# Split products of unchanged activation parts, written to a bank that nobody reads, in six waits of the norm chains

## The reference

```
lat = lat + mod_l[:, 2] * rms_norm(y_lat, norm_g[i, 1])
h   = modulate(rms_norm(lat, norm_g[i, 2]), mod_l[:, 3], mod_l[:, 4])
lat = lat + mod_l[:, 5] * rms_norm(swiglu(h, ffn_w_in[i], ffn_w_out[i]), norm_g[i, 3])
...
h = x * (1.0 + scale_t) + shift_t;  proj = h @ w_in[l]
x = layernorm(DEEPNORM_ALPHA * x + gate_t * mix, ln1_g[l], ln1_b[l])
h = x * (1.0 + scale_f) + shift_f;  u = causal_dwconv(h @ w_up[l], conv_ffn[l]) + b_conv_ffn[l]
x = layernorm(DEEPNORM_ALPHA * x + gate_f * ffn, ln2_g[l], ln2_b[l])
```

## Time and profile before

| | |
|---|---|
| median of 3 runs | 1017.96 us |
| lowest, highest | 1012.38, 1018.58 us |
| profiled execution, first to last instruction | 1009.4 us |
| mean granted TensorE clock in it | 0.977 |
| TensorE matmul busy | 943.4 us (93%) |
| VectorE busy | 702.2 us (70%) |
| ScalarE busy | 548.3 us (54%) |
| DMA: mean rate, bytes moved | 195 GB/s, 196.78 MB |

### The profile page before, as it was taken

The page is one execution under the profiler, slowest core; times in us unless marked ns, Lnnn a source line. Parts: engine busy times, 40 slices in busy tenths (PEclk is TensorE's granted clock), DMA queues, the critical chain, the costliest instruction groups (busy, mean ns, idle before and its releaser), DMA issues.

```text
span 1009.4 us, 19912 instructions
## 1 busy us (share of the span) xinstructions
PE 943.4 (93%) x8438; PEld 891.3 (88%) x8438; DVE 702.2 (70%) x1112; ACT 548.3 (54%) x829; POOL 28.5 (3%) x71
## 2 busy tenths in 40 slices
PE   4699999979999999799999999999999799999995
PEld 1479999859999999699888999988899599999994
DVE  2649936757877766797875544466688678988744
ACT  2658232655544543766746344566765566766434
POOL 2100000000000000310100000000000000000000
PEclk9799999999999999899999999999999899999998
DMA  9834664637888888357433437353386345556931
GB/s 332 293 110 131 224 253 169 209 124 248 276 286 302 285 284 304 104 166 253 146 126 107 167 108 202 122 185 129 117 317 230 110 147 188 188 188 191 340 96 42
DMA packets 57400, 196.78 MB, mean 195 GB/s; under 512 B 6096, under 2 KB 10592, under 8 KB 57056
## 3 DMA queue, kind: packets, MB, share of 16 engines
q1 hardware_dynamic: 51840, 187.72, 55.2%
q10 hardware_dynamic: 5216, 7.53, 2.7%
q0 software_dynamic: 256, 0.26, 0.1%
HBM read 194.43 MB, written 1.06 MB: 194 GB/s over the span
## 4 chain that ended last, share of the span: by engine, by line
PE 76%; DVE 15%; ACT 5%; issue 2%; DMA 2%; ACTq 0%; SPq 0%; DVEq 0%
PE panel_banks L402 64%; DVE mix_work L1807 3%; DVE w_lo L1465 3%; PE work_banks L772 2%; ACT w_hi L950 2%; DMA raw<-in_panels 2%; PE work_banks L599 1%; PE work_banks L743 1%; DVE gla_work L1582 1%; DVE raw L1498 1%; PE work_banks L559 1%; PE work_banks L532 1%; PE work_banks L855 1%; PE work_banks L800 1%; ACT gla_work L988 0%
## 5 line engine op out<-in xcount | busy, mean ns | idle before, releaser
L402 PE MATMUL panel_banks<-act_hi,w_hi 128*128 128x256 f32 (+1 forms) x1600 | 461.9, 289 | 23.1 <-DVE w_lo L1465 8.8
L402 PE MATMUL panel_banks<-act_hi,w_lo 128*128 128x256 f32 (+1 forms) x1600 | 453.3, 283 | 0.0
L402 PE MATMUL panel_banks<-act_lo,w_hi 128*128 128x256 f32 (+1 forms) x1600 | 453.3, 283 | 0.0
L1465 DVE TENSOR_TENSOR w_lo<-raw,w_hi 128x1024 fp32r<-128x1024 f32 x260 | 315.4, 1222 | 126.1 <-ACT w_hi L950 123.9
L950 ACT ACTIVATE w_hi<-raw 128x1024 fp32r<-128x1024 f32 x260 | 272.7, 1055 | 152.0 <-PE panel_banks L402 112.5
L402 PEld LDWEIGHTS panel_banks<-act_hi,w_hi 128*128 128x128 f32 x1600 | 304.9, 191 | 36.8 <-issue 22.2
L402 PEld LDWEIGHTS panel_banks<-act_hi,w_lo 128*128 128x128 f32 x1600 | 306.1, 191 | 1.6
L402 PEld LDWEIGHTS panel_banks<-act_lo,w_hi 128*128 128x128 f32 x1600 | 304.9, 191 | 2.1 <-issue 0.5
L402 PE MATMUL panel_banks<-hidden_hi,w_hi 128*128 128x256 f32 x352 | 97.7, 277 | 2.5 <-ACT hidden_hi L1169 2.5
L402 PE MATMUL panel_banks<-hidden_hi,w_lo 128*128 128x256 f32 x352 | 97.4, 277 | 0.0
L402 PE MATMUL panel_banks<-hidden_lo,w_hi 128*128 128x256 f32 x352 | 97.4, 277 | 0.0
(11 more groups left out here) (268 smaller groups left out, 961.5 us busy)
## 6 DMA issues: line engine op xcount, KB each, us to landing
raw<-in_panels SPq DMA_DIRECT2D x356, 512.0 KB, 5.1
mix_work<-delta_rows ACTq DMA_DIRECT2D x2, 1024.0 KB, 14.6
x_t<-in_x ACTq DMA_DIRECT2D x1, 1024.0 KB, 9.3
gla_work<-in_ctx_x ACTq DMA_DIRECT2D x1, 1024.0 KB, 14.2
mix_work<-in_rel_bias ACTq DMA_DIRECT2D x1, 1024.0 KB, 10.0
out_x<-ffn_work SPq DMA_DIRECT2D x4, 256.0 KB, 2.5
mix_work<-in_rel_bias ACTq DMA_DIRECT2D x1, 768.0 KB, 15.7
c_wide<-in_c_rows ACTq DMA_DIRECT2D x1, 512.0 KB, 4.2
```

The costliest lines, as they stand in the source:

```text
L402: ins = pe.matmul(out_, a, b, start=start and p == 0, stop=stop and p == 2, skip_group_check=True)
L1465: dve.tensor_tensor(wlo[:, v_ % PARTS, :], raw[:, u % RAW, :], whi[:, v_ % PARTS, :].bitcast(F32), ALU.subtract)\
```

## The change

A helper is added on PE that issues n split products with the same operands: weights are the first 128 columns of tile 8 of `act_hi`, the moving operand is tile 9, the result goes to the first 256 columns of bank 3 of the work banks, each product starting its own sum. It waits for nothing and raises no semaphore. It is called in six places ("groups" 1 to 6 in order): 20 products before the squares after gla_out and 20 behind them, 30 behind the sums after ffn_out, 18 between the two sums of the layer norm after mix and 18 behind the second, and 18 between the two sums of the last layer norm: 124 in all.

```diff
+            def idle_products(n):
+
+                for _ in range(n):
+                    pe.matmul(MB[:, 3, 0:T], hhi[:, 8, 0:P], hhi[:, 9, :], start=True, stop=True)
+
...
             norm_part("folded", 0, 3, sq2)
 
+            idle_products(20)
             for r in range(4):
                 if r == 0:
                     pe.wait_ge(S("norm_factor"), 2)
                 norm_part("squares", 4, r, sq2, tiles=2)
+            idle_products(20)
 
             for i in range(22):
                 panel(j, single, ready=None if i else "h2_lo")
...
             for r in range(4):
                 norm_part("folded", 4, r, sq2)
-
+            idle_products(30)
 
             for i in range(12):
                 panel(j, single, ready=None if i else "h3_lo")
...
             norm_part("ln_in", 0, 3, sq2, 0, "ln_sum")
+            idle_products(18)
             for r in range(4):
                 norm_part("folded", 8, r, sq2, 1, "ln_var")
+            idle_products(18)
             for i in range(22):
                 panel(j, single, ready=None if i else "h4_lo")
...
             for r in range(4):
                 norm_part("ln_in", 4, r, sq2, 0, "ln_sum")
+            idle_products(18)
             for r in range(4):
                 norm_part("folded", 12, r, sq2, 1, "ln_var")
```

## The result

| | before | after |
|---|---|---|
| median | 1016.03 us (11 runs) | 1005.67 us (11 runs) |
| lowest, highest | 1008.28, 1022.79 us | 999.31, 1017.27 us |
| profiled execution, span | 1009.4 us | 997.6 us |
| mean granted clock in it | 0.977 | 0.992 |

The ratio is 0.9928 with a 95% interval from 0.990 to 0.9956: 7.3 us less (4.5 to 10.2). It is taken from undisturbed executions alone, so it is not the quotient of the two medians.

A forecast was written before the change was run, and what follows sets the result against it. The prediction saw PE's split products as the bound (76% of the chain), with half clock after waits. Its terms, 0 + 0.8 + 1.4 + 1.45 + 0.35 + 1.43 = 5.4 us off the median 1017.96, gave 1012.6 us, range 1009.0 to 1018.0.

The forecast's parts named there:

- The groups hide in their waits, cost zero: All six groups fit in PE's waits at the high clock with 0.7 to 1.1 us to spare; direct cost zero.
- Slower: Rival, chance 0.08: groups start at the low clock and real products stand behind them; 6.2 us lost, 1024.2 us.
- Group 1, nothing: Squares after gla_out: faster PE gains 0, because the logarithm stands behind ACT's conversion of two weight halves.
- Group 2, half of 1.65: First panel of ffn_in: full clock saves up to 1.65 us; half taken, 0.8, as the clock might still fall.
- Group 3, 1.4: First panel of qkv: 1.8 us earlier at high clock, DVE lets the first convolution move 1.05; 1.4 taken (0 to 1.8).
- Group 4, 1.45: Variance products of the first layer norm, for which ACT, DVE, then PE wait: 1.45 us gained (0 to 1.45).
- Group 5, a quarter of 1.4: First panel of up: up to 1.4 us at stake, a quarter taken, 0.35, as the clock might not hold.
- Group 6, 1.43: Variance products of the last layer norm, with only ACT, DVE and stores behind: 1.43 us gained (0 to 1.43).
- I take the gain off the median: Base of the forecast: the gain taken from the median 1017.96 us, 8.6 over the profiled execution, giving 1012.6.
- All of it: Rival, chance 0.12: the panels of groups 2, 3 and 5 hold fully too; 7.7 us gained, 1010.3 us.
- Only the norm products: Rival, chance 0.25: groups 4 and 6 give 2.9 us, the panels' gain is lost to clock falls or DVE; 1015.1 us.
- nothing: Rival, chance 0.10: products do not keep the clock up, the falls having another cause than idle PE; 1018.0 us.

The follow-up runs named there:

- e2: The changed kernel with only groups 1, 2 and 3, both layer norms as before; median 1011.19 us, ratio to before 0.9984.
- e5: The changed kernel plus tiny products of different kinds behind the float32 norm products within gla_out and mix; 1004.25 us in one execution.
- e8: The changed kernel, unchanged, profiled a second time; 1004.73 us in one execution.
- e9: The changed kernel, unchanged, timed again next to the kernel before; median 1005.86 us (10 runs), ratio to before 0.9952.
- e14: The changed kernel, unchanged, profiled again; 1009.41 us in one execution.
- e15: The changed kernel, unchanged, profiled once more; 1010.30 us in one execution.
- e4: The kernel before, unchanged, profiled a second time; 1012.99 us in one execution, span 1011.2.
- e13: The kernel before, unchanged, its fourth profile; 1009.39 us in one execution.
- e1: The changed kernel with only groups 4, 5 and 6, the two layer norms; median 1006.63 us, ratio to before 0.9957.
- e6: The changed kernel with the same number of added products, each moving 32 columns instead of 256; 1019.15 us in one execution.
- e10: The changed kernel with groups of 24, 27, 34, 20, 23, 18 and a tiny product behind each norm product in gla_out and mix; median 1005.21 us, ratio to before 0.9952.
- e11: The kernel before, without groups, plus a tiny product behind each norm product in gla_out and mix; median 1012.56 us, ratio to before 1.0007.

## Why the prediction was right or wrong

**The groups hide in their waits, cost zero: right.** PE still waits 0.66 to 1.07 us behind them; I had 0.7 to 1.1. They are a little longer than forecast: 2.73 us for 20 and 2.50 for 18, the last one's tail in it, against 2.3 and 2.05. The rival "Slower" needed groups that meet the half clock. In the nine profiles with the groups at the size of the change, or with some of them left out, no product of a group ran at half clock.

**Group 1, nothing: right.** The squares are now done at 218.16 (217.03 + 1.13), but the logarithm stands behind ACT's two weight halves as before. It starts 9.65 us behind the start of the last folded norm product in before (221.44 less 211.79) and 9.67 in after (218.78 less 209.11), by the timelines of ACT and PE. Timeline of ACT in after, which answers to the earlier trace rows:

```profile
216.88 1.99 ACT L960 ACTIVATE w_hi<-raw 128x1024 fp32r<-128x1024 f32 x2
218.78 0.46 ACT L974 ACTIVATE rs<-work_banks,eps 128x256 f32<-128x256 f32 x1
```

**Group 2, half of 1.65: too high.** Where it holds it gives 1.5 to 1.6 (ffn_in 121.1 instead of 122.6), the full term. But of the seven profiles with 20 products there (after, e2, e5, e8, e9, e14, e15) it held in one. On average 0.2, not 0.8. The prediction's own sign of being wrong, a clock that still falls at such a place, came here. Group 2 itself ran at full clock in all seven, and PE waited 1.07 us behind it in each; in six of them the clock fell 1 to 3 us after the first product of the panel.

**Group 3, 1.4: right in kind, 0.4 too high.** The first panel is 1.6 shorter in every profile with the group. The prediction bounded this by DVE at 1.05 and took 1.4 all the same. The first convolution now starts 9.25 us after the layer's first product (418.92 less 409.67), against 10.37 before (424.29 less 413.92): 1.1 earlier, the bound. What the first panel gained beyond it is paid back at the other end of the layer: the last three panels grow from 16.32 to between 16.67 and 17.20 us, and the layer as a whole is 0.8 to 1.3 shorter than 73.5. Timeline of DVE in after, the first convolution, then near the end of qkv:

```profile
418.92 2.68 DVE L1817 SCALAR_TENSOR_TENSOR mix_work<-panel_banks,columns,mix_work 128x255 f32<-128x255 f32 x6
...
474.04 1.23 DVE L1475 TENSOR_TENSOR w_lo<-raw,w_hi 128x1024 fp32r<-128x1024 f32 x1 [0.52 <-ACT w_hi L960]
475.18 2.68 DVE L1817 SCALAR_TENSOR_TENSOR mix_work<-panel_banks,columns,mix_work 128x255 f32<-128x255 f32 x6
477.78 1.22 DVE L1475 TENSOR_TENSOR w_lo<-raw,w_hi 128x1024 fp32r<-128x1024 f32 x1
```

DVE's round of two weight halves and six convolution steps takes some 5.47 us a panel, and PE, which is ahead by the gain, runs into it. One profile of before (e4) had 11.32 and 16.69 without any group; the clock came back earlier there. The mean of qkv is 73.26 in the seven profiles without a group there and 72.45 in the eight with 30 to 34 products, so 0.8 is the fairer value and a little of the 1.0 is chance.

**Group 4, 1.45: right.** Mix is 35.5 to 36.0 without it and 34.2 to 34.7 with it. Its four panels run at one pace or the other, which moves it by 0.3; between profiles with the same paces the difference is 1.36 both times (before 35.74 and after 34.38; e13 36.03 and e15 34.67).

**Group 5, a quarter of 1.4: too low.** It held in seven of the eight profiles that have it (not in e1), and gives 1.5 (up 122.6 to 121.1). I had put it beside group 2 as equally open. The prediction leaned on a clock of 1.00 where group 5 begins. That holds for the one profile read: in the other three of before the clock is at 0.50 over the 4 us ahead of up's first product. Why group 5 nearly always holds and group 2 seldom does is not settled. Both ran at full clock in every profile with wide products.

**Group 6, 1.43: right.** The tail is 17.3 to 17.5 without and 16.15 with it, in every profile with 18 products: 1.1 to 1.35.

**The sum, 5.4 us: right in size.** The terms as measured are 1.4 + 1.35 + 1.0 + 0.2 + 1.3 (1.5 in seven of eight) = 5.25. The second timing gave 4.9, the mean span of five profiles of after is 1004.1 and of four of before 1009.1, and the prediction's own figure for "the same kind of execution" was 1004.0. The result's 7.3 holds 5.25 in its interval. That the sum fits so closely is partly luck. Between the groups it was wrong in three places, and the errors nearly cancelled: 0.6 too much for group 2 and 0.4 for group 3, 1 too little for group 5.

**The step that failed: "I take the gain off the median".** The mechanism was right and the gain had the right size; the term that was mis-sized is the base, 1017.96, the median of three runs. The forecast of 1012.6 was 6.9 us too high. The later sets give 1011.37 (25 runs), 1010.54 (9) and 1011.52 (25) for before, 6.4 to 7.4 us under that base. The profiled execution was the better base. A run's time is its span and 1.7 to 1.8 us in every profiled run that has both (999.31 and 997.6; 1012.99 and 1011.2), and its span and up to 3.5 us in some other runs of before; so I estimate that the profiled execution of before took some 1011 us. Its span of 1009.4 lies within the four (1007.6 to 1011.2). Taking 5.4 off 1011.1 gives 1005.7; the prediction gave 1012.6. The prediction had the 8.6 us between median and profile in front of it and named them, and didn't ask which of the two was the unusual one.

The result's own set explains this only in part. With its 11 runs the median of before is still 1016.03. With that base the same sum gives 1010.6, inside the range, and 5 us over what was measured. The two medians of that set are 10.4 us apart, against 4.9 in the second timing, while the median of after hardly moved (1005.67, then 1005.86). So it was before that ran long in the first set. Why is open.

**The range was too narrow for the same reason.** It took "the runs' own spread of 6 us" from three runs. Twenty-five of before spread over 17 us (1005.50 to 1022.64). The profiles show where a part of this comes from: the slower pace (up 4 to 5 us longer, ffn_in 4.6, ffn_out 2.3, down 2.2, each in some executions), and falls of the clock that move about (z is between 49.3 and 53.7 us). The Trainium skill ("TensorE: Matmul & The Clock Gate", What's actually happening) says that the number of slow matmuls at a start varies from run to run, and puts the cost of a ramp under 1% of a typical span. The traces agree with both: group 2 held in one of seven, the first panel of qkv was quick in e4 without any group, and filling the six waits gave about 5 us of 1009. The prediction cited the first of these, but gave it no width in its range.

**The rivals.** "All of it" (7.7 us) comes near to what the profile pair shows in one execution (6.8); over all of them it falls short by group 2 and by DVE in qkv. "Only the norm products" is refuted by up (121.1 against 122.6), "nothing" and "slower" by both timings of the whole change and by the tail. What "slower" describes did happen to the narrow groups 4 and 5 of e6.

## What to carry to other kernels

Where TensorE waits and then does real work at half clock, the wait can be filled with full-width products of data that is there anyway. That may keep the clock up, but not in every execution: here four groups did their part in nearly every profile, one in one of seven, and one had nothing to give. The gain is at most the time that the real work loses at half clock. It came in full where another engine waited for that work (the norm products). Where another engine paced the layer behind it (DVE in qkv), only a part came. Price such a change against the profiled execution's own time, and before taking any median as the base ask how many runs stand behind it. A layer's duration compared over several profiles settles terms of 1 us that the timings of a kernel that scatters by 15 us can't.

## What the runs showed of the hardware that was not expected

- *Two paces of split products at full clock.* In a dense layer a 128x128 by 256 column product starts every 0.1133 us or every 0.1178, and it keeps to one of them for the whole layer: 840 or 809 products in 95 us at granted clock 1.00. A whole layer of 1056 products is some 4.6 us longer at the slower one. Which it will be differed between executions of the same kernel. Inside gla_out and mix the panels behind a float32 norm product were always at the slower one, unless a tiny product stood right behind the norm product. With it they were at the quicker one in gla_out of e10 and e11 and in mix of e5 and e11; in mix of e10, which had begun at the slower pace, only the last panel was. In the table this is worth 0.2 us or less a layer (mix 34.4 and 34.2), and it didn't show in the timings. What sets the pace was not found.
- *Narrow products took nearly the time of wide ones, and the clock fell.* 18 products of 32 columns held PE for 2.27 us, 18 of 256 columns for 2.50; they start 0.112 and 0.120 us apart. Behind the first the clock fell, behind the second it did not (group 6, e6 and after). At half clock the narrow ones start 0.214 us apart (group 5 of e6), as the full-width split products do.
- *The added products start 0.120 us apart*, not the 0.1139 of the stream from which I priced them, and in each group the second starts 0.306 us after the first. With the last one's 0.28 that makes the 2.50, 2.73 and 3.94 us. All of them write the same bank with the same weights; whether that is the reason wasn't tried.
